# Reordering the opening of a two-layer diffusion backbone, and five multiplications in its Hyena stage

## The reference

```
m_lat = silu(c) @ w_mod[i] + b_mod[i]
m_ctx = silu(c_ctx) @ w_mod[i] + b_mod[i]
h     = rms_norm(x, g) * (1 + scale) + shift
y     = (silu(h @ w_gate) * (h @ w_up)) @ w_down
x     = x + 0.5 * gate * rms_norm(y, g_post)
...
x0, x1, v = split(short_conv(h @ w_in, short_w), 3)      # Hyena
u = v * x1
y = (x0 * (long_conv(u, h_fwd, h_bwd) + u * bias)) @ w_out
```

## Time and profile before

| | |
|---|---|
| median of 3 runs | 1364.27 us (1361.87 to 1366.18) |
| the profiled execution: its time, its span | 1361.87 us, 1360.2 us |
| mean granted TensorE clock over the span | 0.995 |
| TensorE busy | 1317.5 us, 97% |
| weight loads busy (they overlap) | 1128.9 us, 83% |
| VectorE busy | 980.2 us, 72% |
| ScalarE busy | 632.2 us, 46% |
| GpSimd busy | 119.1 us, 9% |

### The profile page before, as it was taken

How to read it: one execution, slowest core, us unless ns; L and a number is a source line. 1 busy time by engine, 2 the same in 40 slices (tenths; PEclk the granted TensorE clock), 3 DMA queues, 4 the chain that set the end, 5 groups by cost and what they waited for, 6 DMA issues and landing times.

```text
span 1360.2 us, 21562 instructions
## 1 busy us (share of the span) xinstructions
PE 1317.5 (97%) x7850; PEld 1128.9 (83%) x7850; DVE 980.2 (72%) x1448; ACT 632.2 (46%) x967; POOL 119.1 (9%) x209
## 2 busy tenths in 40 slices
PE   6899999999999999999999999999999999999997
PEld 3678777887778988788999989999877888899996
DVE  5788776887767785667888578886765687865554
ACT  6533332323456565564444464444355434644443
POOL 3000010111000421011111001100000000000000
PEclk9899999999999999999999999999999999999999
DMA  9445666677645653269888649866543435665662
GB/s 361 190 170 181 210 208 235 241 254 265 215 142 184 185 162 101 80 209 337 300 301 282 205 133 337 306 225 179 156 123 107 128 113 195 229 182 184 187 189 96
DMA packets 76360, 275.13 MB, mean 202 GB/s; under 512 B 9226, under 2 KB 9781, under 8 KB 75712
## 3 DMA queue, kind: packets, MB, share of 16 engines
q1 hardware_dynamic: 52128, 187.00, 42.0%
q0 software_dynamic: 24160, 87.12, 18.8%
HBM read 273.04 MB, written 1.05 MB: 202 GB/s over the span
## 4 chain that ended last, share of the span: by engine, by line
PE 88%; DVE 5%; ACT 3%; DMA 1%; issue 1%; SPq 0%; ACTq 0%; DVEq 0%
PE gu L1641 17%; PE gu L1643 17%; PE gu L1642 17%; PE acc L1702 8%; PE acc L1704 8%; PE acc L1703 8%; DMA wlo<-in_wstream_dram 1%; PE acc L1691 1%; DVE wlo_r L993 1%; PE acc L2101 1%; ACT whi L609 1%; PE acc L1977 1%; DVE z L1087 1%; PE acc L1988 1%; PE acc L1955 1%
## 5 line engine op out<-in xcount | busy, mean ns | idle before, releaser
L1641 PE MATMUL gu<-h_hi,whi 128*128 128x256 f32 (+1 forms) x1744 | 537.3, 308 | 8.3 <-DVE h_lo L1118 7.2
L1642 PE MATMUL gu<-h_lo,whi 128*128 128x256 f32 (+1 forms) x1744 | 531.1, 305 | 0.0
L1643 PE MATMUL gu<-h_hi,wlo_r 128*128 128x256 f32 (+1 forms) x1744 | 530.8, 304 | 0.0
L993 DVE TENSOR_TENSOR wlo_r<-wlo,whi 128x1024 fp32r<-128x1024 f32 x350 | 421.4, 1223 | 100.8 <-ACT whi L609 99.0
L609 ACT ACTIVATE whi<-wlo 128x1024 fp32r<-128x1024 f32 x350 | 359.8, 1049 | 86.2 <-DMA wlo<-in_wstream_dram 85.9
L1641 PEld LDWEIGHTS gu<-h_hi,whi 128*128 128x128 f32 x1744 | 329.4, 189 | 37.6 <-issue 9.0
L1642 PEld LDWEIGHTS gu<-h_lo,whi 128*128 128x128 f32 x1744 | 329.6, 189 | 20.5 <-issue 2.2
L1643 PEld LDWEIGHTS gu<-h_hi,wlo_r 128*128 128x128 f32 x1744 | 330.0, 189 | 15.5
L1010 DVE SCALAR_TENSOR_TENSOR part<-wm,cvec,part 128x512 f32<-128x512 f32 x266 | 199.4, 750 | 6.7
L1702 PE MATMUL acc<-whi,act_hi 128*128 128x512 f32 x440 | 176.4, 401 | 4.8 <-DVE act_lo L1188 4.8
L1704 PE MATMUL acc<-wlo_r,act_hi 128*128 128x512 f32 x440 | 174.8, 397 | 0.0
(11 more groups left out here) (333 smaller groups left out, 1172.6 us busy)
## 6 DMA issues: line engine op xcount, KB each, us to landing
wlo<-in_wstream_dram SPq DMA_DIRECT2D x350, 512.0 KB, 3.6
wm<-in_wmod_dram POOLq DMA_DIRECT2D x132, 512.0 KB, 5.8
area<-in_wmod_dram POOLq DMA_DIRECT2D x11, 512.0 KB, 19.9
z<-in_gate_rows_dram POOLq DMA_DIRECT2D x6, 512.0 KB, 7.1
gate_keep<-in_gate_rows_dram POOLq DMA_DIRECT2D x5, 512.0 KB, 6.5
area<-in_rpb_dram POOLq DMA_DIRECT2D x32, 64.0 KB, 3.8
x_lat<-in_x_in_dram SPq DMA_DIRECT2D x1, 1024.0 KB, 7.6
area<-in_ctx_in_dram SPq DMA_DIRECT2D x1, 1024.0 KB, 9.0
```

The costliest lines, as they stand in the source:

```text
L993: nc.vector.tensor_tensor(wlo[:, u.base % RING, :], raw[:, u.base % RING, :], whi[:, u.base % RING, :].bitcast(F32), ALU.subtract).then_in ...
L1641: nc.tensor.matmul(out_, w_hi, x_hi, start=start, stop=False, skip_group_check=True)
L1642: nc.tensor.matmul(out_, w_hi, x_lo, start=False, stop=False, skip_group_check=True)
L1643: return nc.tensor.matmul(out_, w_lo, x_hi, start=False, stop=stop, skip_group_check=True)
```

## The change

Three queues of the opening are put in another order, and the table of the Hyena steps is changed. No instruction is added or taken away. On TensorE, `ahead(0)` is no longer interrupted by the latent `norm_columns`; `ahead_columns(0)` stands ahead of `ahead(1)`; both context `norm_columns` stand ahead of `ahead_columns(1)`; and the first latent tiles stand ahead of `ahead_columns(2)`. On VectorE, `chunk_lo(4)` moves ahead of the copies to `z`, chunks 6 and 7 behind `ahead_out(0)`, the splits of units 0 and 1 ahead of `first_los(0)`, chunks 10 and (with it) 11 behind `first_los(0)`, and the splits of units 2 and 3 one step forward. ScalarE's queue follows. In the Hyena stage steps (1, 2) and (1, 3) move from unit 21 to unit 22, and (1, 4) to (1, 6) to unit 23.

```diff
@@ ScalarE
             for n in range(1, 6):
                 chunk_hi(n)
+            row(0)
             square(1, 0)
             square(1, 1)
-            for n in (6, 7):
-                chunk_hi(n)
-            row(0)
-            for n in (8, 9):
+            for n in range(6, 10):
                 chunk_hi(n)
             row(1)
-            for n in (10, 11, 12):
-                chunk_hi(n)
-            h_his(0, range(4))
             for u in range(2):
                 split_hi(u, u)
+            h_his(0, range(4))
+            for n in range(10, 14):
+                chunk_hi(n)
             row(2)
-            for n in (13, 14, 15):
+            for n in range(14, 16):
                 chunk_hi(n)
             h_his(1, HI_ORDER[:4])
             row(3)
+            for u in (2, 3):
+                split_hi(u, u)
             h_his(0, range(4, KT))
-            split_hi(2, 2)
             h_his(1, HI_ORDER[4:])
-            split_hi(3, 3)
             load_table(ACT.Silu)
@@ VectorE
-            for n in range(1, 4):
+            for n in range(1, 5):
                 chunk_lo(n)
             for b in range(4):
                 v.wait_ge(hp_done, b + 1)
                 nc.vector.tensor_copy(z[:, 2 * b:2 * b + 2, :].rearrange("p a b -> p (a b)"), acc[:, b, :]).then_inc(xt_copied, 1)
-            chunk_lo(4)
             chunk_lo(5)
             spread(1, 0)
             spread(1, 1)
-            chunk_lo(6)
-            chunk_lo(7)
             ahead_out(0)
-            for n in (8, 9, 10):
+            for n in range(6, 10):
                 chunk_lo(n)
             ahead_out(1)
+            for u in range(2):
+                split(Unit(u))
             first_coef(0, 0)
             first_coef(1, 0)
             first_los(0)
-            chunk_lo(11)
-            for u in range(2):
-                split(Unit(u))
-            chunk_lo(12)
-            chunk_lo(13)
+            for n in range(10, 14):
+                chunk_lo(n)
             ahead_out(2)
             first_coef(0, 1)
             first_coef(1, 1)
-            chunk_lo(14)
-            chunk_lo(15)
+            for n in range(14, 16):
+                chunk_lo(n)
             second_los(0)
+            split(Unit(2))
             ahead_out(3)
             first_los(1)
-            split(Unit(2))
+            split(Unit(3))
             second_los(1)
-            split(Unit(3))
@@ TensorE
-            ahead(0, (0, 1))
+            ahead(0)
             norm_columns(0, 0)
             norm_columns(0, 1)
-            ahead(0, range(2, KT))
-            ahead(1)
             pe.wait_ge(picked, 1)
             ahead_columns(0)
+            ahead(1)
             norm_columns(1, 0)
+            norm_columns(1, 1)
             ahead_columns(1)
-            norm_columns(1, 1)
             ahead(2)
+            first_tiles(LAT, range(0, 4))
             ahead_columns(2)
-            first_tiles(LAT, range(0, 4))
             ahead(3)
@@ Hyena
 YF_AT = {13: [(0, 0)], 14: [(0, 1)], 15: [(0, 2), (0, 3)], 16: [(0, 4), (0, 5), (0, 6)],
-         20: [(1, 0)], 21: [(1, 1), (1, 2), (1, 3), (1, 4)], 22: [(1, 5), (1, 6)]}
+         20: [(1, 0)], 21: [(1, 1)], 22: [(1, 2), (1, 3)], 23: [(1, 4), (1, 5), (1, 6)]}
```

More of the change, by code:

```diff
@@ L1773, in ffn, with ahead @@
                             ffn_turn(Unit(u0, j), j * 2 + n0, j * 2 + a0, (j + (t0 - 1), None) if i <= jobs else None, xs)
-            def ahead(l, kts=range(KT)):
+            def ahead(l):
                 rows_ = ahead_bank(l)
@@ L1780, in ahead @@
                     pe.wait_ge(mod_ready, l - 1)
-                for kt in kts:
+                for kt in range(KT):
                     n, cols = 4 * l + kt // 2, slice(kt % 2 * 512, kt % 2 * 512 + 512)
```

## The result

The changed kernel takes 1373.94 us (median of 4 runs, 1373.38 to 1375.94), the kernel before took 1365.22 (4 runs) beside it. The ratio is 1.0068, with a 95% interval of 1.0049 to 1.0088: slower by 6.7 to 12.0 us. The profiled execution has a span of 1371.9 us, against 1360.2. I forecast 1375 and a range of 1370 to 1380.

What follows compares the result with a forecast made beforehand. The prediction took TensorE, without a gap in the windows, as the bound, so its stalls move the end. Opening 7.0 plus Hyena 3.9 made 10.9 us, from the median 1364.27 to 1375; range 1370 to 1380.

Steps and rivals of the forecast that it cites:

- Up to `ahead_out(1)`: Opening's first part: latent columns end at 24.3 instead of 17.15, and `ahead_out(1)` comes at 35.4, 4.0 us late.
- Chunk 10: Opening: queued behind splits and `first_los(0)`, it reaches TensorE at 43.05 after 5.9 us of standing, at the lower clock.
- Return of the pace: Opening, after chunk 10's restart: the upper clock level returns after 3.8 or 6.0 us, called the unknown.
- my three values: Opening: ScalarE may start chunk 15 5.8, 6.8 or 7.9 us late, depending on when the pace rises; 6.8 taken.
- 45.94: Opening: the start of chunk 15's high part on ScalarE in the earlier trace, base for its forecast delay.
- The tail: Opening from chunk 15 on: splits add 0.2 us, the Silu table load gives nothing; opening total 7.0 us.
- The Hyena wait: Hyena stage: TensorE stands 3.9 us for step (1, 4) before the projection's token half 1, from 1125.62 to 1129.5.
- The sum: Whole kernel: 7.0 us for the opening plus 3.9 for the Hyena stage, 10.9 us slower.
- The 2.83 us of the earlier trace: Opening: time read for 24 later matmuls between 59.02 and 61.85, 0.118 each, as the upper clock level.
- the 5.28: Opening: time read for 24 latent tile matmuls from 39.05, 0.22 each, as the lower clock level.
- the 0.50 at 40 us of the earlier trace: Opening: granted clock cited as agreeing with the rule that a long wait leaves matmuls at the reduced clock.

Runs made afterwards that it cites:

- chunks_ahead: opening_only with both parts of chunks 10 and 11 back ahead of first_los(0) and the splits of units 0 and 1: 0.9997 of the kernel before.
- opening_only: The changed kernel's opening with the old table of Hyena steps: 1.0043 of the kernel before, 5.9 us slower.
- hyena_only: The kernel before, old opening kept, with the changed table of Hyena steps: 1.0040 of the kernel before, 5.4 us slower.
- the fillers: Idle matmuls put into TensorE's wait: on opening_only 44 (1.0068) or 25 (1.0045), on hyena_only 30 (1.0052) or 16 (1.0022), against the kernel before.
- all_chunks_first: The kernel before with the latent tiles of blocks 0 to 3 moved behind ahead(3) on TensorE: 1.0005 of the kernel before.
- step4_earlier: The kernel before with the new Hyena table, except step (1, 4) taken back from unit 23 to unit 22: 1.0017, 2.3 us slower.
- chunks_first_tuned: The kernel before with the opening's second half reordered, several moves at once, including all of ahead(3) ahead of the latent tiles: 1357.84 us, 0.9965.
- columns_first: opening_only with ahead_columns(1) ahead of the context norm_columns on TensorE: 1.0020 of the kernel before.
- latent_early: opening_only with the latent norm_columns behind chunk 0 again, ahead of chunks 1 to 3: 1.0022 of the kernel before.

## Why the prediction was right

The mechanism held at both places, step by step. The number was helped by luck in its sizes, as the last points say.

- **Up to `ahead_out(1)`.** Forecast at 35.4, seen at 35.43. Latent columns end at 24.2, forecast 24.3. TensorE's first matmul came 0.26 later in the changed profile than in the one of before (10.71 against 10.45), so the agreement is one of some 0.3 us.
- **Chunk 10.** Forecast at 43.05, seen at 42.98 with a wait of 5.64, at the lower level. chunks_ahead shows that without this queueing the opening loses nothing. Taken back alone, the late `ahead_columns(1)` gave 3.1 and the unbroken `ahead(0)` 1.3, with chunks 10 and 11 queued behind them; with those two chunks put back, both moves stayed in and the opening was as long as the old one.
- **Return of the pace.** This term was mis-sized. I took the middle of my three values, 6.8 us late for chunk 15, with the level back 6.0 us after the restart; it rose 4.1 us after it, near the lower bound (3.8), and chunk 15 was 5.85 late. My 6.0 came from the profiled execution of before, in which the lower level lasted longer than in the four others. The same execution was the base of 45.94, so against the usual old opening chunk 15 is later than that: 41.1 us after the first matmul instead of 33.9 to 34.4, or 6.7 to 7.1. So 6.8 came out right against that base by two errors that met.
- **The tail.** I counted nothing for the Silu table load. Its move under the tiles gave 0.4: the silu's wait went from 0.83 to 0.42. The first full turn came 5.5 late instead of 7.0. Against the usual length of the old opening it is 6.4 to 6.8, and by the time of opening_only it is 5.9 (4.0 to 7.8).
- **The Hyena wait.** Forecast 3.9, seen 3.71. Here I left a term out: I had applied the lower pace to the opening's wait and not to this one. From half 1's first matmul to `inverse(4)` it adds 1.4 in the changed kernel (5.53 - 4.11) and 1.7 in hyena_only (5.84 - 4.11), and the fillers show that it comes from standing: with TensorE at work in the wait the clock stayed at 1.00.
- **The sum.** 10.9 forecast, 8.7 between the medians, 11.7 between the spans. The two errors (opening 1.5 too high, Hyena 1.4 too low) cancel in the profile, which is luck; 1.1 of the 11.7 is the transfer above. That 1375 lies 1.1 from the measured 1373.94 is closer than the forecast difference deserves: 10.9 is inside the interval of 6.7 to 12.0, but 2.2 above the difference of the medians, and the median that I started from, 1364.27, was 0.95 lower than the one measured beside the changed kernel.
- **Readings that were off.** The 2.83 us of the earlier trace rows is from the first to the last of 24 starts, so 23 spacings, against 24 in the 5.28; nothing hangs on it. And the 0.50 at 40 us of the earlier trace rows is no example of a low clock behind a long wait: TensorE's last waits ahead of it were 0.47 and 0.68 us.

The Trainium skill's rule that a long wait between matmuls leaves TensorE at the lower clock ("TensorE: Matmul & The Clock Gate", Loop structure matters more than you think) is told there for a wait on a DMA. It held at both places here, where TensorE waited for VectorE: this trace agrees, with 0.50 granted after 5.64 us and after 3.71 us of standing. That the level turns again some way into sustained activity stands on the same page of the Trainium skill, under What you observe; here it came back 4.1 us after the restart in the opening and some 2.8 in the projection.

## What to carry to other kernels

When three in-order queues feed each other, ask of a moved block what is now queued behind it and who waits for that: here 5.6 us of VectorE work ahead of one 1.2 us subtraction cost the opening its 6.4 to 6.8 us, and putting chunks 10 and 11 back ahead of it repaired that although every other move stayed. A stand of the bounding engine also has a tail, the slower pace after it, which belongs in the sum of every wait of some microseconds. And before moving a step out of a stand, look for the next wait behind it: twice the gain was taken by the next one in line, wholly in all_chunks_first and in part in step4_earlier. In the opening it took the move of the next ones as well to keep it (chunks_first_tuned).

## What was not expected of the hardware

- The granted clock fell without a long stand of TensorE. In columns_first a stand of 1.97 us came before it, while in the kernel before 1.91 us at 57 us did not bring it down. And in the kernel before it fell at about 38.4, with TensorE at work in the whole microsecond and waits of only 0.47 and 0.68 us ahead; in chunks_ahead it stayed at 1.00 there. What decides is left open. The row is from the kernel before, with the columns of the earlier trace rows:

```profile
38.00:39.00 1.00, 1.00 (x8) 1.00 (x7) 1.00 (x2) 1.00 (x2) 0.00 (x0) 0.70 1.00 397
```

- The time at the lower level after a restart differed between runs of like work: 4.2 us in opening_only, 5.7 in latent_early. In the first the level had set in 2.6 us ahead of chunk 10, in the second 1.2 us. With the same old opening it moved the opening by 1.1 to 1.5 us from profile to profile.
- In the first 20 us the trace says 1.00 for the granted clock, while 512-column matmuls start 0.43 apart as at 0.50 later (from 16.04 to 19.8 in the changed kernel): there the spacing has to be read, not the clock.
